# Gate one-hots and gates in FP16, a gate as a scaled high and low part, summed in PSUM

## What is computed

```
q = (xt @ w_query).reshape(T, H, 2, PEER_HALF)
s = jnp.einsum('thcd,cnd->thcn', q, sub_keys).astype(jnp.float32)
sv, si = lax.top_k(s, K)
cand_s = (sv[:, :, 0, :, None] + sv[:, :, 1, None, :]).reshape(T, H, K * K)
cand_i = (si[:, :, 0, :, None] * PEER_NKEYS + si[:, :, 1, None, :]).reshape(T, H, K * K)
top_s, pos = lax.top_k(cand_s, K)
idx = jnp.take_along_axis(cand_i, pos, axis=-1)
gate = jax.nn.softmax(top_s, axis=-1)
a = jnp.einsum('thkd,td->thk', down[ib], xb).astype(jnp.float32)
c = (gb * jax.nn.gelu(a)).astype(up.dtype)
out = jnp.einsum('thk,thkd->td', c, up[ib])
```

## Time and profile before

| | us |
|---|---|
| median of 3 runs | 2859.25 |
| lowest and highest | 2859.18, 2859.89 |
| profiled execution, first to last instruction (span) | 2858.0 |
| TensorE busy, matmul (17542 instructions) | 2840.0 (99%) |
| TensorE busy, weight loads | 2542.5 (89%) |
| VectorE busy | 1988.3 (70%) |
| ScalarE busy | 1511.6 (53%) |

### The profile page before, as it was taken

One profiled execution on the slowest core, in us unless ns is written; L12 is line 12 of the kernel. 1 busy time (PEld: TensorE's weight loads), 2 busy tenths in 40 slices (PEclk: granted clock), 3 DMA queues, 4 the chain that ended last, 5 costly groups with the idle time before them and its releaser, 6 DMA issues.

```text
span 2858.0 us, 44352 instructions
## 1 busy us (share of the span) xinstructions
PE 2840.0 (99%) x17542; PEld 2542.5 (89%) x17542; DVE 1988.3 (70%) x3010; ACT 1511.6 (53%) x2219; POOL 113.5 (4%) x81
## 2 busy tenths in 40 slices
PE   8999999999999999999999999999999999999998
PEld 7899988889999899999888999988899988888997
DVE  7889999655555788999966555566655556665664
ACT  6644874544444575488454444445455444545543
POOL 0033000000000002400000000000000000000000
PEclk9999999999999999999999999999999999999999
DMA  6344556765554534455676554556555656554663
GB/s 215 119 163 164 195 190 204 278 250 179 178 201 164 177 111 163 142 209 181 214 280 243 191 191 176 187 179 185 182 166 180 188 187 185 170 184 155 176 186 133
DMA packets 223376, 530.13 MB, mean 185 GB/s; under 512 B 13514, under 2 KB 87408, under 8 KB 211952
## 3 DMA queue, kind: packets, MB, share of 16 engines
q1 hardware_dynamic: 221872, 521.11, 54.8%
q0 software_dynamic: 1344, 6.82, 0.7%
HBM read 507.81 MB, written 20.06 MB: 185 GB/s over the span
## 4 chain that ended last, share of the span: by engine, by line
PE 98%; DVE 1%; DMA 0%; issue 0%; ACT 0%; SPq 0%; DVEq 0%
PE ps L2650 16%; PE ps L2632 13%; PE ps L1518 13%; PE ps L1528 12%; PE ps L1506 12%; PE ps L1446 9%; PE ps L1463 5%; PE ps L602 4%; PE ps L593 4%; PE ps L1435 2%; PE ps L2909 2%; PE ps L1236 1%; PE ps L2818 0%; PE ps L2802 0%; PE ps L1348 0%; DMA common_sb<-in_common 0%
## 5 line engine op out<-in xcount | busy, mean ns | idle before, releaser
L2251 DVE TENSOR_TENSOR ring_lo<-ring,w_hi 128x1024 fp32r<-128x1024 f32 x320 | 388.4, 1224 | 242.9 <-ACT w_hi L2247 241.7
L2247 ACT ACTIVATE w_hi<-ring 128x1024 fp32r<-128x1024 f32 x320 | 335.2, 1056 | 235.4 <-PE ps L2650 168.7
L1518 PE MATMUL ps<-h_t_lo,down_hi 128*128 128x256 f32 x1024 | 288.2, 281 | 0.0
L1518 PE MATMUL ps<-h_t_expert,down_lo 128*128 128x256 f32 x1024 | 287.8, 281 | 0.0
L1518 PE MATMUL ps<-h_t_expert,down_hi 128*128 128x256 f32 x1024 | 286.8, 280 | 0.0
L1446 PE MATMUL ps<-h_t,ring 128*128 128x256 f32 x1216 | 283.5, 379 | 0.0
L2632 PE MATMUL ps<-h_t_lo,w_hi 128*128 128x256 f32 x928 | 260.7, 281 | 0.0
L2632 PE MATMUL ps<-h_t_hi,w_hi 128*128 128x256 f32 x928 | 259.4, 280 | 0.1
L2632 PE MATMUL ps<-h_t_hi,ring_lo 128*128 128x256 f32 x928 | 259.0, 279 | 0.0
L1446 PEld LDWEIGHTS ps<-h_t,ring 128*128 128x128 f32 x1216 | 221.1, 190 | 24.9
L1122 ACT ACTIVATE out_hi<-ring 128x1024 fp32r<-128x1024 f32 x128 | 135.6, 1060 | 159.2 <-PE ps L1506 153.1
(11 more groups left out here) (522 smaller groups left out, 7225.2 us busy)
## 6 DMA issues: line engine op xcount, KB each, us to landing
ring<-in_peer_down SPq DMA_DIRECT2D x128, 1024.0 KB, 5.1
ring<-in_w_in SPq DMA_DIRECT2D x140, 512.0 KB, 3.7
ring<-in_peer_up SPq DMA_DIRECT2D x68, 1024.0 KB, 4.8
ring<-in_w SPq DMA_DIRECT2D x132, 512.0 KB, 3.7
ring<-in_peer_up SPq DMA_DIRECT2D x120, 512.0 KB, 4.3
late_gates<-arena SPq DMA_DIRECT2D x64, 256.0 KB, 4.2
arena<-late_gates SPq DMA_DIRECT2D x16, 1024.0 KB, 6.9
ring<-in_w_out SPq DMA_DIRECT2D x16, 512.0 KB, 3.9
```

The source lines that it names most:

```text
L1518: m = pe.e.matmul(PS[:, 4 + b, j * T:(j + 1) * T], w[:, b, o], x[:, kc, :], start=kc == 0 and n == 0, stop=kc == KD - 1 and n == 2)
L2247: a.e.activation(W_HI[:, g % HI_SLOTS, :], RAW[:, g % RAW_SLOTS, :], ACT.Copy).then_inc(*a.count(f"c{g}_hi"))
L2251: v.e.tensor_tensor(RAW_LO[:, g % RAW_SLOTS, :], RAW[:, g % RAW_SLOTS, :], W_HI[:, g % HI_SLOTS, :].bitcast(F32), ALU.subtract).then_inc(* ...
```

## The change

Both one-hots, the mask and the gate's parts are stored in FP16 instead of FP32R, FP32 and BF16. A gate is multiplied by 2^14, rounded to FP16 as the high part, and the rest, again in FP16, is the low part. Each token now has two matmuls of 128 columns with the same weights: mask times high part, then mask times low part, the second added to the first in PSUM. So a call is eight matmuls, one PSUM bank holds four tokens, and the banks are used in turn, four deep. ScalarE's copy out of PSUM is the only one left and carries the scale 2^-14; VectorE's sum is gone. Both products of mask and gate are on VectorE, with the operands written as pairs of FP16; ScalarE's scaled copies are gone. `MASK` has two slots. Sizes in SBUF are kept by a filler (`odd_room`).

```diff
-GATE_BANKS = (0, 2, 6)
+GATE_BANKS = (0, 1, 2, 3)
+GATE_SCALE = 2.0 ** 14
...
-        with nc.sbuf_tensor("hot_first", [P, 2, GROUP, P], F32R) as HOT1, \
-                nc.sbuf_tensor("hot_mask", [P, GROUP, P], BF16) as MASK:
+        with nc.sbuf_tensor("hot_first", [P, 2, GROUP, P], F16) as HOT1, \
+                nc.sbuf_tensor("hot_mask", [P, 2, GROUP, P], F16) as MASK:
...
-            def hot_high(n):
-
-                a.e.wait_ge(*a.at(f"mask{n}"))
-                if n >= 2:
-                    a.e.wait_ge(*a.at(f"sum{2 * n - 3}"))
-                for j in range(GROUP):
-                    at = n * GROUP + j
-                    a.e.activation(HOT2[n % 2][:, j, 0, :], MASK[:, j, :], ACT.Copy,
-                                   scale=PARTS[:, at, 0:1].bitcast(F32)) \
-                        .then_inc(*a.count(f"hot_high{n}" if j == GROUP - 1 else None))
-
-            def gates_high(s):
+            def gates_out(s):
...
-                a.e.activation(gates_of(s), gate_sums(s, 0), ACT.Copy).then_inc(*a.count(f"high{s}"))
+                a.e.activation(gates_of(s), gate_sums(s), ACT.Copy, scale=1.0 / GATE_SCALE).then_inc(*a.count(f"gates{s}"))
...
-                n, bank = s // 2, GATE_BANKS[s % 3]
+                n, banks = s // 2, len(GATE_BANKS)
                 if s % 2 == 0:
                     pe.e.wait_ge(*pe.at(f"hot_low{n}"))
-                    pe.e.wait_ge(*pe.at(f"hot_high{n}"))
-                if s >= 3:
-                    pe.e.wait_ge(*pe.at(f"low{s - 3}"))
+                if s >= banks:
+                    pe.e.wait_ge(*pe.at(f"gates{s - banks}"))
                 for j in range(FEW):
-                    k, at = s % 2 * FEW + j, j % 2 * T
-                    m = pe.e.matmul(PS[:, bank + j // 2, at:at + T], HOT1[:, n % 2, k, :],
-                                    HOT2[n % 2][:, k, :, :].rearrange("p i n -> p (i n)"), start=True, stop=True)
+                    k = s % 2 * FEW + j
+                    for part in range(2):
+                        m = pe.e.matmul(PS[:, GATE_BANKS[s % banks], j * P:(j + 1) * P], HOT1[:, n % 2, k, :],
+                                        HOT2[n % 2][:, k, part, :], start=part == 0, stop=part == 1)
                 m.then_inc(*pe.count(f"sum{s}"))
...
-            def gates_low(s):
-
-                v.e.wait_ge(*v.at(f"high{s}"))
-                v.e.tensor_tensor(gates_of(s), gate_sums(s, 1), gates_of(s), ALU.add).then_inc(*v.count(f"low{s}"))
-
...
+                v.e.tensor_tensor(paired(MASK[:, n % 2, :, :]), pairs, each(HK_SECOND[:, at:at + GROUP, :]), ALU.is_equal) \
+                    .then_inc(*v.count(f"mask{n}"))
                 if n >= 2:
                     v.e.wait_ge(*v.at(f"sum{2 * n - 3}"))
-                v.e.tensor_tensor(HOT1[:, n % 2, :, :], numbers, each(HK_FIRST[:, at:at + GROUP]), ALU.is_equal) \
+                v.e.tensor_tensor(paired(HOT1[:, n % 2, :, :]), pairs, each(HK_FIRST[:, at:at + GROUP, :]), ALU.is_equal) \
                     .then_inc(*v.count())
...
-                v.e.tensor_tensor(HOT2[n % 2][:, :, 1, :], MASK[:, :, :], each(PARTS[:, at:at + GROUP, 1].bitcast(F32)),
-                                  ALU.mult).then_inc(*v.count(f"hot_low{n}"))
+                for part in range(2):
+                    v.e.tensor_tensor(paired(HOT2[n % 2][:, :, part, :]), paired(MASK[:, n % 2, :, :]),
+                                      each(PARTS[:, part, at:at + GROUP, :]), ALU.mult) \
+                        .then_inc(*v.count(f"hot_low{n}" if part else None))
...
-                v.e.tensor_copy(PARTS[:, o, 0], PS[:, t, 2 * P:3 * P]).then_inc(*v.count())
-                v.e.tensor_copy(HK_FIRST[:, o], PS[:, t, 0:P]).then_inc(*v.count())
+                gates = PS[:, t, 2 * P:3 * P].unsqueeze(2).broadcast_to([P, P, 2])
+                v.e.tensor_scalar(PARTS[:, 0, o, :], gates, GATE_SCALE, None, ALU.mult).then_inc(*v.count())
+                v.e.tensor_copy(HK_FIRST[:, o, :], PS[:, t, 0:P].unsqueeze(2).broadcast_to([P, P, 2])).then_inc(*v.count())
...
-                v.e.tensor_tensor(PARTS[:, o, 1], PS[:, t, 2 * P:3 * P], PARTS[:, o, 0].bitcast(F32), ALU.subtract) \
+                v.e.scalar_tensor_tensor(PARTS[:, 1, o, :], gates, GATE_SCALE, PARTS[:, 0, o, :], ALU.mult, ALU.subtract) \
...
-                        sp.e.wait_ge(*sp.at(f"low{2 * n + 1}"))
+                        sp.e.wait_ge(*sp.at(f"gates{2 * n + 1}"))
```

More of the change, by code:

```diff
@@ L14 @@
 U32 = mybir.dt.uint32
-BF16 = mybir.dt.bfloat16
+F16 = mybir.dt.float16
 I32 = mybir.dt.int32
@@ L349, in build @@
         COMMON = sb("common_sb", [P, N_COMMON])
-        with nc.sbuf_tensor("hot_second0", [P, GROUP, 2, P], F32R) as HOT2_EVEN:
+        with nc.sbuf_tensor("hot_second0", [P, GROUP, 2, P], F16) as HOT2_EVEN:
             pass
@@ L373, in build @@
             pass
-        HOT2_ODD = sb("hot_second1", [P, GROUP, 2, P], F32R)
-        with nc.sbuf_tensor("hk_first", [P, T], F32) as HK_FIRST, nc.sbuf_tensor("hk_second", [P, T, 2], BF16) as HK_SECOND, \
-                nc.sbuf_tensor("gate_parts", [P, T, 2], F32R) as PARTS:
+        with nc.sbuf_tensor("hot_second1", [P, GROUP, 2, P], F16) as HOT2_ODD:
+            pass
+        sb("odd_room", [P, 2 * GROUP * P])
+        with nc.sbuf_tensor("hk_first", [P, T, 2], F16) as HK_FIRST, nc.sbuf_tensor("hk_second", [P, T, 2], F16) as HK_SECOND, \
+                nc.sbuf_tensor("gate_parts", [P, 2, T, 2], F16) as PARTS:
             pass
@@ L408, in build @@
         HT_HI = sb("h_t_hi", [P, KD, T], F32R)
-        NUMBERS = sb("numbers", [P, P], BF16)
+        NUMBERS = sb("numbers", [P, P], F16)
         PS = ctx.enter_context(nc.psum_tensor("ps", [P, 8, 512], F32))
@@ L686, in gates_of, with gate_sums @@
                            ap=[whole.ap[0], [late - early, 2], [64, FEW], [1, 64]])
[L688 to L692, removed]
+        def gate_sums(s):
+            return PS[:, GATE_BANKS[s % len(GATE_BANKS)], :].rearrange("p (k h n) -> p h k n", k=FEW, h=2)
         def raw(which, slot):
@@ L1096, in hybrid_scalar @@
                 if n >= 2:
-                    gates_high(2 * n - 3)
+                    gates_out(2 * n - 3)
                     acts_out(2 * n - 3)
@@ L1105, in hybrid_scalar @@
                 if n:
-                    gates_high(2 * n - 2)
+                    gates_out(2 * n - 2)
                     if n > 1:
                         acts_out(2 * n - 2)
-            gates_high(SUMS - 1)
+            gates_out(SUMS - 1)
             def high(which, slot, name):
@@ L1959, in hybrid_vector @@
             choice_gates(v)
-            def gates_low(s):
-                v.e.wait_ge(*v.at(f"high{s}"))
-                v.e.tensor_tensor(gates_of(s), gate_sums(s, 1), gates_of(s), ALU.add).then_inc(*v.count(f"low{s}"))
             def hot(n):
                 at = n * GROUP
-                numbers = IOTA.unsqueeze(1).broadcast_to([P, GROUP, P])
-                halves = NUMBERS[:, :].rearrange("p (a b) -> p a b", b=2).unsqueeze(1).broadcast_to([P, GROUP, P // 2, 2])
-                second = HK_SECOND[:, at:at + GROUP, :].unsqueeze(2).broadcast_to([P, GROUP, P // 2, 2])
+                pairs = NUMBERS[:, :].rearrange("p (a b) -> p a b", b=2).unsqueeze(1).broadcast_to([P, GROUP, P // 2, 2])
@@ L1973, in each, with paired @@
                 def each(ap):
-                    return ap.unsqueeze(2).broadcast_to([P, GROUP, P])
+                    return ap.unsqueeze(2).broadcast_to([P, GROUP, P // 2, 2])
+                def paired(ap):
+                    return ap.rearrange("p j (a b) -> p j a b", b=2)
+                v.e.tensor_tensor(paired(MASK[:, n % 2, :, :]), pairs, each(HK_SECOND[:, at:at + GROUP, :]), ALU.is_equal) \
+                    .then_inc(*v.count(f"mask{n}"))
                 if n >= 2:
                     v.e.wait_ge(*v.at(f"sum{2 * n - 3}"))
-                v.e.tensor_tensor(HOT1[:, n % 2, :, :], numbers, each(HK_FIRST[:, at:at + GROUP]), ALU.is_equal) \
+                v.e.tensor_tensor(paired(HOT1[:, n % 2, :, :]), pairs, each(HK_FIRST[:, at:at + GROUP, :]), ALU.is_equal) \
@@ L2005, in hybrid_vector @@
                     lead_low(v, LEAD + 1, 1)
-            for s in range(SUMS - 4, SUMS):
-                gates_low(s)
-            v.e.wait_ge(*v.mine())
+            v.e.wait_ge(*v.at(f"gates{SUMS - 1}"))
             fold(0, 1)
@@ L2215, in choice_gates @@
                 o = slice(t * P, (t + 1) * P)
[L2216 to L2217 removed]
+                gates = PS[:, t, 2 * P:3 * P].unsqueeze(2).broadcast_to([P, P, 2])
+                v.e.tensor_scalar(PARTS[:, 0, o, :], gates, GATE_SCALE, None, ALU.mult).then_inc(*v.count())
+                v.e.tensor_copy(HK_FIRST[:, o, :], PS[:, t, 0:P].unsqueeze(2).broadcast_to([P, P, 2])).then_inc(*v.count())
                 v.e.tensor_copy(HK_SECOND[:, o, :], PS[:, t, P:2 * P].unsqueeze(2).broadcast_to([P, P, 2])).then_inc(*v.count())
                 v.e.wait_ge(*v.mine(2))
[L2220 removed]
```

(2 more changed lines are left out.)

2 lines of the change are left out of this document (removed).

## The result

| | before | after |
|---|---|---|
| median of 20 runs, us | 2859.95 | 2864.26 |
| lowest and highest, us | 2859.09, 2861.98 | 2862.88, 2866.38 |
| span of the profiled execution, us | 2858.0 | 2861.8 |
| TensorE busy (matmul), us | 2840.0 | 2844.3 |
| VectorE busy, us | 1988.3 | 1882.3 |

The changed kernel is slower by 4.3 us; the ratio is 1.0014, with an interval of 1.0008 to 1.0021. The forecast was 2858.0 us, 1.3 us faster than the 2859.25 (median of 3 runs) that it started from. It took 5.7 us as the least that a measurement of this kernel can tell from no change; with 20 runs of each, 4.3 us are clear.

What follows compares the result with a forecast made beforehand. TensorE, busy 99% of the span, was taken as the bound, VectorE and ScalarE savings worth 0. Gate matmuls: -60.4 + 59.1 = -1.3 on 2858.0 gives 2856.7, plus the 1.25 median difference, 2858.0 us; range 2855 to 2882.5.

Steps and rivals of the forecast that it cites:

- The 4-byte form of VectorE's operations: Rival in the gate stage: four VectorE operations of 1.22 us make TensorE wait 31 us, 2889 us; chance 0.02.
- The ways in and out: Start and end of the gate stage: first group ready at 276.3, output products not delayed; all priced at 0.
- The pace of the products: Gate matmuls of 128 columns in 16 bit: 57.7 ns each, 1024 taking 59.1 us against 60.4 before.
- the bounds: Limits for the 16-bit gate matmul's pace: 54.0 ns from the stream alone, 111.7 ns with a 4-byte-like load.
- the value taken: Pace assumed for each 16-bit gate matmul, from the key product's 32 matmuls in 2.06 us: 57.7 ns.
- the ceiling: Gate matmul with a load as dear as 4-byte: 111.7 ns, 54.0 us more, 2913.3 us; chance near it 0.08.
- The line through FP32R (62 ns): Gate matmul pace from FP32R at 256 and 512 columns: 62 ns for 128, so 63.5 us, 3.1 more.
- The rival in which the 16-bit load is exposed, at 80 ns or more: Gate matmuls: load and stream add up to about 80 ns, 22.8 us more, 2880.8 us; chance 0.20.
- The step that failed: End of each gate call: FP32 load behind the last 16-bit matmul costs nothing; otherwise 50 ns x 128 calls, 6.4 us.

## Why the prediction was wrong

The bound was read rightly: TensorE alone, no wait in the stage, VectorE and ScalarE worth 0 (the window, the waits, and the version with VectorE's products doubled). The 4-byte form of VectorE's operations did not come; they take 0.685 us. The ways in and out held: the first group's last operation on VectorE ends at 274.36 (forecast: by 276.3), and held_lo at 421.73 stands 1.4 us ahead of the output products.

The pace of the products was well inside the bounds, though lower than the value taken: 55.9 ns instead of 57.7, so they give 3.2 us and not 1.3. That it came so close is luck, because the earlier trace rows were misread. The key products do not come one by one with a load each 57.7 ns; they come in pairs, as narrow windows of the kernel before show:

```profile
182.17 0.38 PE L1415 MATMUL ps<-keys,arena 64*128 64x128 f32 x2 [0.29 <-DVE arena L1950]
182.38 0.39 PE L1415 MATMUL ps<-keys,arena 64*128 64x128 f32 x4
182.49 0.39 PE L1415 MATMUL ps<-keys,arena 64*128 64x128 f32 x4
```

Two products lie within 0.38 us though each lasts 0.373 (the longest of the earlier trace rows), so they start together; two start at 182.38 and the next two at 182.49. So each half of the rows has a product about every 0.11 us, near the 111.7 ns of the ceiling, and 57.7 is half of that and some time at the start. The row said nothing on a product with a load of its own in 16 bit. The line through FP32R (62 ns) misled as well: FP16 takes 256 columns in 109 ns where FP32R needs 118, and FP32R takes 128 in 111.8. The rival in which the 16-bit load is exposed, at 80 ns or more, did not come about within the products.

The step that failed is this one: "By the earlier trace rows the next matmul starts 50 ns into its load, so this costs nothing; if it did, it would be 50 ns x 128 calls = 6.4 us." It does cost that: 56 ns behind each of 128 calls, 7.2 us, and so the kernel became slower and not faster. The 4-byte load was exposed, not the 16-bit one. The mistake was to take the start of a matmul's record for the start of its stream. The earlier trace rows show a matmul recorded 50 ns after its load, and the changed kernel shows the same: the FP32 group is recorded at 284.34, 0.44 us after the first gate product. But the first of its instructions is recorded for 0.43 us and not 0.38, and the second follows after 0.27 and not 0.216, so the first began its record on time and delivered late. The same rows held the answer in another form: if the FP32 matmuls over 64 columns need 111.7 ns with a stream of 54, then 58 ns of a 4-byte load behind a stream of 54 are exposed, and the FP32 instruction behind a call is just that case. I used that row as a ceiling for the products and not for the neighbour.

With this term in its place the sum would have been -1.3 + 6.4 = +5.1 us, 2864.4. That this nearly equals the 2864.26 measured is luck in part: the measured terms are -3.2 and +7.2, and the 20 runs of the kernel before have a median 0.7 us above the 2859.25 that the forecast started from. The time lies inside the forecast's range of 2855 to 2882.5 us, but the range was drawn that wide for 16-bit loads that are not hidden, and these were hidden.

The Trainium skill's page TensorE: Matmul & The Clock Gate, section Back-to-back issue gap, gives two figures. The 81 ns for a sustained stream of loads and matmuls of 128 columns is not borne out: the trace has 55.9 ns, in pieces of 8 to 32 products. The same section's figure for a single gap, 128 columns at about 56 ns, agrees. Its section Weight-path perf modes says that a fast weight load applies to 128 weights that are not FP32; the 98 ns recorded for the 16-bit load beside 190 for the 4-byte one agree with that for FP32 and FP16, though no run shows whether that mode was on; the version with one-hots in FP32R records its loads with 187 to 193 ns, as FP32.

What is shown and what is not: the excess goes with the ends, not with the products, and all but 2 or 3 ns of it disappear when the last stream of a call has 256 columns. The load's own records say that it is the weight load: from one FP32 load to the next it takes 110 ns behind a product of 128 columns and behind one of 256, and 110 less the 54 of the stream is the 56 measured. No run varied the length of the load at the end alone.

## What to carry to other kernels

A matmul's price has two sides: its own stream, and how much of its successor's weight load it covers. When a long product is cut into short ones, or moved to 16 bit, look at what stands behind the last of them; a 4-byte load behind a 54 ns stream cost 56 ns here, 128 times. Where both are wanted, keep the wide product (FP16 over 256 columns: 2855.8 us, below both kernels, while VectorE has room for the sums; this was measured without the factor of 2^14) or do the short ones in longer pieces (four calls at a time: 2858.9). For prices close to each other, read rounds of the pipeline from start to start over a whole period, and not the start of a single record; over two rounds alone, rows given to 0.01 us leave some 5 ns open. And before a row is taken as a pace, look whether its instructions start one by one or in pairs.

## What was not expected of the hardware

- The record of a matmul can start some 50 ns after its load's, whether or not it can deliver then; the delay appears in the length of that record (0.43 instead of 0.38 us) and in the start of the next.
- FP16 keeps 109 ns over 256 columns, FP32R 118 (the version with the wide product against the kernel before), so a product of this size takes 9 ns longer in FP32R. No run shows why.
- Products on the two halves of the rows run at the same time: the key products start in pairs, a pair every 0.11 us or a little less.
- Two 16-bit products with their loads, the second adding to the first in the same 128 columns of PSUM, keep 55.9 ns. So do the single products with new weights each time (2.005 us a round with four of them): neither the sum in PSUM nor the repeated load of the same weights slows them.
